# Hybrid decoder block: the attention values taken with the value block as weights, the probabilities scaled before they are turned, z multiplied ahead of the masks

## The reference, cut to what matters

```python
# attention: each query sees 128 keys back, plus one sink logit per head
scores = jnp.einsum('bnqgrd,bnkgd->bgrnqk', qb, kk)      # masked to the band
m      = jnp.maximum(jnp.max(scores, axis=-1, keepdims=True), sink)
pexp   = jnp.exp(scores - m)
probs  = pexp / (jnp.sum(pexp, axis=-1, keepdims=True) + jnp.exp(sink - m))
out    = jnp.einsum('bgrnqk,bnkgd->bnqgrd', probs, vv)
# SSD: y is the sum of a part within the chunk of 128 tokens and a part from the carried state
g = y * jax.nn.silu(z)                                   # z = u @ w_z
g = g * lax.rsqrt(jnp.mean(g * g, axis=-1, keepdims=True) + NORM_EPS)   # per group of 512
```

## Time and profile before

| | |
|---|---|
| median of 3 runs | 2165.03 us (2163.56 to 2168.50) |
| profiled execution | 2168.98 us, its span 2167.4 us |
| PE busy | 2090.6 us (96%) |
| VectorE / ScalarE / GpSimd busy | 1307.5 / 844.0 / 598.4 us |
| mean granted TensorE clock | 0.984 |
| `mixers` | 32 steps, 19.7 us each in the middle of a group |

### The profile page before, as it was taken

One profiled execution on the slowest core, in us unless ns is written; L12 is line 12 of the kernel. 1 busy time (PEld: TensorE's weight loads), 2 busy tenths in 40 slices (PEclk: granted clock), 3 DMA queues, 4 the chain that ended last, 5 costly groups with the idle time before them and its releaser, 6 DMA issues. The chain is left out here.

```text
span 2167.4 us, 29054 instructions
## 1 busy us (share of the span) xinstructions
PE 2090.6 (96%) x10218; PEld 1739.7 (80%) x10218; DVE 1307.5 (60%) x1824; ACT 844.0 (39%) x1589; POOL 598.4 (28%) x600
## 2 busy tenths in 40 slices
PE   7999999979999999999979999999999999999997
PEld 6888889967878778778758888887888888878885
DVE  6854552237767767777743344558887777752523
ACT  5332221024454444454443222434444443443432
POOL 1000011146576666565610000004222222100000
PEclk9999999989999999999989999999999999999998
DMA  6122241223443433443355434321222222355343
GB/s 225 62 90 97 87 166 69 84 85 129 119 125 117 124 114 124 124 131 97 95 175 179 141 134 145 122 94 72 88 87 71 75 87 87 138 161 195 112 151 88
DMA packets 131264, 252.73 MB, mean 117 GB/s; under 512 B 25264, under 2 KB 70448, under 8 KB 131152
## 3 DMA queue, kind: packets, MB, share of 16 engines
q1 hardware_dynamic: 85584, 174.98, 24.9%
q0 software_dynamic: 15360, 55.32, 7.5%
q10 hardware_dynamic: 30208, 20.98, 3.0%
HBM read 189.63 MB, written 61.60 MB: 116 GB/s over the span
## 5 line engine op out<-in xcount | busy, mean ns | idle before, releaser
L155 PE MATMUL ps_zg<-u_hi,g_hi 128*128 128x512 f32 x448 | 186.0, 415 | 0.0
L157 PE MATMUL ps_zg<-u_hi,g_lo 128*128 128x512 f32 x448 | 177.1, 395 | 0.0
L156 PE MATMUL ps_zg<-u_lo,g_hi 128*128 128x512 f32 x448 | 176.2, 393 | 0.0
L2057 DVE TENSOR_TENSOR lt_d_lo<-lt_w_raw,lt_d_hi 128x640 fp32r<-128x640 f32 (+1 forms) x64 | 57.1, 892 | 147.2 <-ACT lt_d_hi L1782 142.5
L973 POOL TENSOR_TENSOR mx_seg<-mx_seg,mx_cbm 128x1024 f32<-128x1024 f32 x32 | 76.0, 2376 | 161.3 <-DVE mx_cbm L1130 161.3
L155 PE MATMUL ps_zg<-z_w,u_hi 128*128 128x512 f32 x256 | 108.6, 424 | 7.1 <-DVE mx_silu L1155 6.9
L155 PE MATMUL lt_ps<-lt_h_hi,lt_w_hi 128*128 128x512 f32 x256 | 100.7, 393 | 14.8 <-DVE lt_h_lo L2095 13.6
L157 PE MATMUL ps_zg<-z_w,u_lo 128*128 128x512 f32 x256 | 102.3, 400 | 0.0
L156 PE MATMUL ps_zg<-z_w,u_hi 128*128 128x512 f32 x256 | 101.8, 398 | 0.0
L1782 ACT ACTIVATE lt_d_hi<-lt_w_raw 128x640 fp32r<-128x640 f32 (+1 forms) x64 | 50.6, 791 | 130.5 <-PE lt_ps L157 119.6
L1656 POOL TENSOR_TENSOR lt_t_f<-lt_w_raw 128x512 f32<-128x512 f32 x21 | 29.1, 1385 | 261.7 <-DVE lt_t_lo L1985 260.2
(11 more groups left out here) (390 smaller groups left out, 6229.8 us busy)
## 6 DMA issues: line engine op xcount, KB each, us to landing
lt_w_raw<-in_w_up SPq DMA_DIRECT2D x44, 512.0 KB, 4.5
mx_a_row<-acs_s SPq DMA_DIRECT2D x32, 512.0 KB, 3.9
g_raw<-in_w_xbc SPq DMA_DIRECT2D x24, 512.0 KB, 3.2
lt_sig<-gate_s SPq DMA_DIRECT2D x24, 512.0 KB, 3.6
lt_w_raw<-in_w_down SPq DMA_DIRECT2D x32, 384.0 KB, 3.2
ff_s<-lt_fo SPq DMA_DIRECT2D x21, 512.0 KB, 5.0
tok_s<-fr_work POOLq DMA_DIRECT2D x20, 512.0 KB, 3.8
lt_w_raw<-in_w_down SPq DMA_DIRECT2D x32, 320.0 KB, 2.9
```

The costliest lines, as they stand in the source:

```text
L155: pe.matmul(dst, s_hi, m_hi, start=first, stop=False)
L156: pe.matmul(dst, s_hi, m_lo, start=False, stop=False)
L157: return pe.matmul(dst, s_lo, m_hi, start=False, stop=last)
L2057: dve.tensor_tensor(d_lo[:, m % 2, 0:n], w_raw[:, m % 2, 0:n], d_hi[:, m % 2, 0:n].bitcast(F32), ALU.subtract).then_inc(dw_lo_done, 1)
```

## The change

The probabilities are scaled by `rden` before they are turned, by four ScalarE copies. So the product with the values needs no division afterwards, and it can be taken the other way round: the value block (64 columns) is the weights, two heads' turned probabilities (256 columns) the moving side, two such pairs go to the two halves of the partitions of `ps_f`, and what comes out is already turned. VectorE's `attention_out`, its tile `o_tok` and PE's L1261 go. The values stand behind gate 0 to 3 instead of ahead of it. The probabilities are turned after all of z instead of after z 2. On ScalarE the sigmoid's exp goes ahead of the splits and output copies; on VectorE silu(z) goes ahead of the gate split and the masks, and `rden` from behind the gated y to just behind the state update.

```diff
@@ ScalarE
-                act.wait_ge(o_turned, n + 1)
+                act.wait_ge(pv_done, n + 1)
...
                     act.activation(silu[:], silu[:], ACT.Ln, bias=one[:]).then_inc(z_ln_done, 1)
+                    act.wait_ge(z_ln_done, n + 1)
+                    act.activation(silu[:], silu[:], ACT.Exp, scale=-1.0).then_inc(z_sig_done, 1)
                     if c % 2 == 1 and not (last and c == NT - 1):
...
                         outputs(g if c else g - 1, (c - 1) % NT, first and c <= 2)
-                    act.wait_ge(z_ln_done, n + 1)
-                    act.activation(silu[:], silu[:], ACT.Exp, scale=-1.0).then_inc(z_sig_done, 1)
                     act.wait_ge(max_ready, n + 1)
                     keys = P if c == 0 else 2 * P
                     for r in range(REP):
-                        ins = act.activation(sc[:, r, 0:keys], sc[:, r, 0:keys], ACT.Exp, bias=negm[:, r:r + 1],
-                                             accum_out=sums[:, r:r + 1])
-                    ins.then_inc(exp_done, 1)
+                        act.activation(sc[:, r, 0:keys], sc[:, r, 0:keys], ACT.Exp, bias=negm[:, r:r + 1],
+                                       accum_out=sums[:, r:r + 1])
...
                         for k in range(4, KT):
                             split_z(g + 1, k)
+                    act.wait_ge(rden_ready, n + 1)
+                    for r in range(REP):
+                        ins = act.activation(sc[:, r, 0:keys], sc[:, r, 0:keys], ACT.Copy, scale=rden[:, r:r + 1])
+                    ins.then_inc(p_scaled, 1)
                     act.wait_ge(p_turned, n + 1)
@@ VectorE
-                    if not opening:
-                        attention_out(n - 1, first and c == 1)
...
                     dve.tensor_tensor(cbm[:], ps_d[:, 0:P], utri[:], ALU.mult).then_inc(cbm_ready, 1)
+                    dve.wait_ge(z_sig_done, n + 1)
+                    dve.tensor_tensor(silu[:], ps_z[:], silu[:], ALU.mult).then_inc(z_used, 1)
...
-                    dve.wait_ge(z_sig_done, n + 1)
-                    dve.tensor_tensor(silu[:], ps_z[:], silu[:], ALU.mult).then_inc(z_used, 1)
-
...
                         dve.tensor_tensor(state[:], kept[:], ps_f[:], ALU.add).then_inc(state_ready, 1)
+                    dve.wait_ge(sink_done, n + 1)
+                    if not opening:
+                        dve.wait_ge(p_scaled, n)
+                    do(dve.tensor_tensor(rden[:], sums[:], sink_e[:], ALU.add))
+                    dve.reciprocal(rden[:], rden[:]).then_inc(rden_ready, 1)
                     dve.wait_ge(diag_done, n + 1)
...
-                    dve.wait_ge(sink_done, n + 1)
-                    do(dve.tensor_tensor(rden[:], sums[:], sink_e[:], ALU.add))
-                    do(dve.reciprocal(rden[:], rden[:]))
@@ PE
+                n = NT * g + c
+                pe.wait_ge(p_ready, n + 1)
+                if c < NT - 1:
+                    pe.wait_ge(state_ready, (NT - 1) * g + c + 1)
+                else:
+                    pe.wait_ge(o_out, n)
                 j, blocks = c % 2, 1 if c == 0 else 2
-                for r in range(REP):
-                    for b in range(blocks):
-                        block_of = c if b == j else c - 1
-                        last = pe.matmul(ps_a[:, r * HD:(r + 1) * HD], p_t[:, r, b], v_in[:, block_of % 4],
+                for b in range(blocks):
+                    block_of = c if b == j else c - 1
+                    for h in range(2):
+                        last = pe.matmul(ps_f[h * HD:(h + 1) * HD, 0:2 * P].rearrange("p (a n) -> p a n", a=2),
+                                         v_in[:, block_of % 4], p_t[:, 2 * h:2 * h + 2, b],
                                          start=(b == 0), stop=(b == blocks - 1))
                 last.then_inc(pv_done, 1)
...
                     if not opening:
+                        gate(g, c, range(0, 4), opening)
                         values(*before)
-                    if not opening:
-                        gate(g, c, range(0, 4), opening)
...
-                    if not opening:
-                        pe.wait_ge(o_ready, n)
...
-                    next_z(g, c, last_group, range(0, 3))
-                    pe.wait_ge(exp_done, n + 1)
+                    next_z(g, c, last_group, range(KT))
+                    pe.wait_ge(p_scaled, n + 1)
                     for r in range(REP):
                         for b in range(keys // P):
                             last = pe.transpose(ps_s[:, r // 2, r % 2, b * P:(b + 1) * P], sc[:, r, b * P:(b + 1) * P], ident[:])
                     last.then_inc(p_turned, 1)
-                    next_z(g, c, last_group, range(3, KT))
```

More of the change, by code:

```diff
@@ L831, in mixers @@
         p_t = s.sb("p_t", [P, REP, 2, P])
-        o_tok = s.sb("o_tok", [P, REP * HD])
         o_t = s.sb("o_t", [P, 2, 2, P])
@@ L853, in mixers @@
             s.sem(n) for n in "gated sq_done v_ready r0_ready yn_ready y_turned y_out".split())
-        rotated, qk_turned, q_ready, scored, masked, max_ready, exp_done, sink_done, p_turned, p_ready, pv_done, o_ready, o_turned, o_out = (
-            s.sem(n) for n in "rotated qk_turned q_ready scored masked max_ready exp_done sink_done p_turned p_ready pv_done o_ready o_turned o_out".split())
+        rotated, qk_turned, q_ready, scored, masked, max_ready, sink_done, rden_ready, p_scaled, p_turned, p_ready, pv_done, o_out = (
+            s.sem(n) for n in "rotated qk_turned q_ready scored masked max_ready sink_done rden_ready p_scaled p_turned p_ready pv_done o_out".split())
         dve_own, pool_own, act_own = s.sem("dve_own"), s.sem("pool_own"), s.sem("act_own")
@@ L1096, in split_gate @@
                 dve.tensor_tensor(g_lo[:, w], g_raw[:, w], g_hi[:, w].bitcast(F32), ALU.subtract).then_inc(g_lo_done, 1)
-            def attention_out(n, opening):
-                dve.wait_ge(pv_done, n + 1)
-                if not opening:
[L1102 to L1106, removed]
             def group(g, first, last):
@@ L1194, in group @@
                 assert own.n == OWN
-            OWN = 8 * NT + 2 * (NT - 1) + (NT - 2)
+            OWN = 7 * NT + 2 * (NT - 1) + (NT - 2)
             group(0, True, False)
@@ L1200, in _ @@
             group(NG - 1, False, True)
-            attention_out(NG * NT - 1, False)
         @block.tensor
@@ L1236, in values @@
             def values(g, c):
-                pe.wait_ge(p_ready, NT * g + c + 1)
-                j, blocks = c % 2, 1 if c == 0 else 2
-                for r in range(REP):
-                    for b in range(blocks):
-                        block_of = c if b == j else c - 1
-                        last = pe.matmul(ps_a[:, r * HD:(r + 1) * HD], p_t[:, r, b], v_in[:, block_of % 4],
+                n = NT * g + c
[4 more added lines that the diff above has]
+                    pe.wait_ge(o_out, n)
+                j, blocks = c % 2, 1 if c == 0 else 2
+                for b in range(blocks):
[3 more added lines that the diff above has]
+                                         v_in[:, block_of % 4], p_t[:, 2 * h:2 * h + 2, b],
                                          start=(b == 0), stop=(b == blocks - 1))
@@ L1254, in turn_outputs @@
                 last.then_inc(y_turned, 1)
-                pe.wait_ge(o_ready, n + 1)
-                if c < NT - 1:
-                    pe.wait_ge(state_ready, (NT - 1) * g + c + 1)
-                else:
-                    pe.wait_ge(o_out, n)
-                for a in range(2):
-                    last = pe.transpose(ps_f[:, a * P:(a + 1) * P], o_tok[:, a * P:(a + 1) * P], ident[:])
-                last.then_inc(o_turned, 1)
             def group(g, first, last_group):
```

## The result

| | before | after |
|---|---|---|
| median of 15 runs each | 2167.25 us | 2172.40 us (2167.83 to 2176.61) |
| ratio, with its 95% interval | | 1.0024 (1.0017 to 1.0031), or +5.2 us |
| profiled execution, its span | 2168.98, 2167.4 us | 2170.32, 2168.7 us |
| PE busy | 2090.6 us | 2069.1 us |
| VectorE / ScalarE / GpSimd busy | 1307.5 / 844.0 / 598.4 us | 1251.8 / 887.5 / 595.4 us |

The kernel is slower by 5.2 us, where 8.4 had been forecast, while TensorE is busy for 21.5 us less. A second measurement of the same kernel gave 1.0019 (1.0010 to 1.0028), or +4.1 us. The two profiled executions differ by only 1.3 us of span. A second profiled execution of the changed kernel had a span of 2173.6, +6.2.

A forecast was written before the change was run, and what follows sets the result against it. TensorE was taken as the bound in the middle of a group, 19.74 us a step. Terms of -4.8, -0.6, +1.3, +9.0 and +3.5 gave +8.4 on a median of 2165.03, so 2173.4 us; range 2160 to 2191.

The forecast's parts named there:

- 12 even steps: Even steps in the middle of a head group take 19.27 us, 0.4 less than now: -4.8 us together.
- 12 odd steps: Odd steps take 19.8 us against 19.85, with `rden` held up by GpSimd's decays: -0.6 us together, bounds 19.3 and 20.9.
- 3 first steps: In each group's first step the scores come later and only half the values go: +0.45 us each, +1.3 together.
- 3 last steps of a group: VectorE's low halves of z 4 to 7 come later, TensorE idles some 6 us: +3.0 each, bounds 1 and 5.
- the end, less the first step: The last step, with no z to hide anything, is 4.3 us later; less 0.8 for the first step: +3.5.
- The values: On TensorE, eight records of 256 columns in two column halves take 1.15 us instead of 1.70; bounds 0.86 and 2.0.
- The chain ahead of the scores: From transposes through norm, decays and copies of q and k, scores start at 7.17; TensorE waits 0.35 us every step.
- the sign that the chain is shorter than I read: Steps at 19.0 us in the profile after would show the forecast wrong about the wait ahead of the scores.
- rival B: In odd steps GpSimd's loads land 1 us later and `rden` meets only short operations: -5.7 us, 2159.3; chance 0.14.
- rival D: Chain ahead of the scores 0.3 shorter (even steps 18.97), last steps of a group +2: +1 us, 2166; chance 0.13.

The follow-up runs named there:

- run 1: Changed kernel with both head pairs sent to partitions 0 to 63, so the column halves can't work side by side: 2185.13 us, ratio 1.0083.
- Run 4: Changed kernel with the decays' clamp ahead of the previous step's norm and their exp behind its square: 2159.68 us, ratio 0.9956.
- run 10: Kernel before with only the four-column maximum operations in PSUM, the sink sum staying in SBUF: 2164.22 us, ratio 0.9986.
- run 6: Changed kernel with the maximum of the scores and the sink's exponential held in PSUM: 2158.41 us, ratio 0.9968.
- run 8: Changed kernel with the decays' clamp and exp done a step early, and the maximum and sink's exponential in PSUM: 2143.66 us, ratio 0.9890.

## Why the prediction was right, and where it was not

The forecast was +8.4 (2173.4 us), in a range of 2160 to 2191; the time came out at 2172.4 (+5.2), and at +4.1 in the second measurement. The reason given was that TensorE's gain in the loop is eaten by the group ends and the end. That is what the tables show. Term by term, with the first trace:

| term | forecast | measured |
|---|---|---|
| 12 even steps | -4.8 | -8.4 |
| 12 odd steps | -0.6 | -5.1 |
| 3 first steps | +1.3 | +0.4 (second trace +2.8) |
| 3 last steps of a group | +9.0 | +9.7 |
| the end, less the first step | +3.5 | +4.4 |
| sum | +8.4 | +1.0 (second trace +4.6) |

- *The values* were put at 1.15, with 0.86 and 2.0 as ends; they take 1.02. The analogy to the scores' two halves held, and run 1 shows what it was worth: 0.85 a step.
- *The chain ahead of the scores* was the right bound. It was to be 7.17 from the transposes and is 7.03 (546.35 - 539.32): the copy to `p_t` starts 0.06 earlier (540.39), and the clamp follows it after 3.69 (544.08), not 3.76. Behind the scores it is 11.95 for 12.1. So even steps are 18.97 instead of 19.27; the announced idle ahead of the scores was 0.35, and is 0.11 to 0.15. I had named 19.0 as the sign that the chain is shorter than I read, and so it is, by 0.14. Run 4 took the chain away and found the 0.2.
- *Odd steps* are the term that failed: -0.05 forecast, -0.42 measured. The step of the working that was wrong is the start of the masks, 10.55 after the gate. I took the 4.04 from q's copy to the masks from the earlier trace rows, and in them lies VectorE's gate split as it ran beside GpSimd. In the new order GpSimd's mix has ended (8.2 after the gate) when the split begins, and it takes 1.23 instead of 1.98. First the rows of before (GpSimd and VectorE, the step of the earlier trace rows), then those of after, an odd step from 559.09:

```profile
687.39 2.38 POOL L973 TENSOR_TENSOR mx_seg<-mx_seg,mx_cbm 128x1024 f32<-128x1024 f32 x1 [4.57 <-DVE mx_cbm L1130]
...
688.87 1.98 DVE L1096 TENSOR_TENSOR g_lo<-g_raw,g_hi 128x1024 fp32r<-128x1024 f32 x1 [1.62 <-ACT g_hi L1018]
```

```profile
564.91 2.38 POOL L972 TENSOR_TENSOR mx_seg<-mx_seg,mx_cbm 128x1024 f32<-128x1024 f32 x1 [2.92 <-ACT mx_seg L1028]
...
566.58 0.69 DVE L1122 TENSOR_TENSOR mx_silu<-ps_zg,mx_silu 128x512 f32<-128x512 f32 x1 [2.30 <-ACT mx_silu L1039]
567.53 1.23 DVE L1098 TENSOR_TENSOR g_lo<-g_raw,g_hi 128x1024 fp32r<-128x1024 f32 x1 [0.26 <-ACT g_hi L1017]
568.67 1.28 DVE L1132 SCALAR_TENSOR_TENSOR mx_sc<-mx_ps_s,band 128x512 f32<-128x512 f32 x2
...
574.35 0.16 DVE L1160 TENSOR_TENSOR mx_rden<-mx_sums,mx_sink_e 128x4 f32<-128x4 f32 x1 [0.32 <-ACT mx_sink_e L1053]
...
574.95 1.91 POOL L954 TENSOR_TENSOR mx_seg<-mx_a_row,mx_acs_g 128x1024 f32<-128x1024 f32 x1
```

  Masks start 9.58 after the gate, and `rden` at 15.26 (16.4 forecast), with GpSimd's decays at 15.86. The sum gets through 0.6 us ahead of the decays, and takes 0.16. This is rival B's place, and nearly its gain (-5.1 against -6.6), though not by its mechanism: GpSimd was no later than I had put it (decays at 16.2 after the gate; they came at 15.0 to 16.1), but VectorE was earlier. It is a near miss: in seven of the twelve steps the sum starts less than 0.1 us ahead of the decays, and in three more it starts behind them and takes 1.25 to 1.30.
- *Group ends* had the right size, +3.25 each on average for +3.0 (2.6, 2.1 and 5.0), from partly other parts. Halves at 19.5 (20.6 forecast, less the one microsecond by which the masks came sooner); 5.07 long, not 3.00, which I had taken from the earlier trace rows without asking what GpSimd would do beside them by then; and an idle of 5.2 for 6 in the step shown, of which 1.76 stands ahead of L1284 and not ahead of z 4, where all 6 had been put. What I had missed altogether is why they are late. I knew the collision of small operations from the earlier trace rows and looked for it at `rden` only; the maximum's two operations had it in the step of the earlier trace rows already, and my working moved it along unseen. It cost 5.7 us at the three group ends of the kernel before (run 10) and costs 9.7 in the changed one (run 6), whose group ends without it take as long as those of the kernel before (73.70 and 73.63).
- *The end*: the last transposes start 15.96 after their gate, against 11.23, so 4.7 later for 4.3. Most of the rest of the 0.9 over the forecast is the transposes at the lower clock, 1.79 for 1.09. The slow values cost nothing: they end at 1101.81, and TensorE's next work, the turn of y, starts at 1102.58, when VectorE's norm is done.

That the total landed within 3.2 us of the forecast is in part luck. Steps c = 0 to 6 gained 9.0 more than the terms gave them (-13.1 for -4.1), while the group ends and the end lost 1.6 more. By the first trace the sum is rival D's (+1.0), and D's chain, 0.3 shorter, is what the even steps show, though not its +2 at the group ends. The medians lie between D and the forecast. Part of the gap between trace and median is which executions were profiled: that of before lies 1.7 above its median (2168.98 for 2167.25), the first of after 2.1 below (2170.32 for 2172.40), the second 5.1 above (2175.17 for 2170.07). Why executions of one kernel differ is only partly seen. The second trace is 3.6 longer than the first in the table, and steps n = 16 and n = 9 alone are 3.7 longer (21.00 for 18.65, 21.94 for 20.62). In n = 16 TensorE waits 2.29 ahead of the scores, in the first trace not at all. I have no run that fixes how far GpSimd and VectorE have come when that step starts.

## What to carry to other kernels

When work moves off the bounding engine, list each wait that it used to cover, with the chain that will end last there; here TensorE was busy for 21.5 us less and the program got slower, until two such chains were shortened; with them shortened the same change was worth about 20 us (runs 8 and 10). A duration taken from a row carries the neighbours that ran beside it: ask of each what GpSimd did then, and what it will do in the new order, for tiny operations above all. Cures found one at a time need not go together: the two reorderings that made 3 us with a late maximum cost 6.6 with an early one.

## What the runs showed of the hardware

- A VectorE `tensor_tensor` on 128x4 with both inputs in SBUF took 0.16 us or up to 1.85 us, by GpSimd's operation beside it, and a `tensor_scalar` 0.17 or up to 1.21; with one operand in PSUM they always took 0.15 to 0.17 (runs 6 and 8). The low half of the gate weights (128x1024) took 1.23 clear of GpSimd's mix and 1.98 where it met it. The row maximum over 128x1024 took 1.22 either way.
- The clock multiplies a wait. After 3.48 us idle, z 4 to 7 took 5.65 at a granted clock of 0.52, against 3.19 at 1.00 in run 8. It is not a matter of the longest idle alone: in run 6 a group's end with one idle of 1.75 had a mean clock of 0.85. In run 8 one with 2.32 and 0.93 had 1.00, and the next one, with 2.33 and 0.93, had 0.93. What decides between these can't be said from these traces.
- Eight fp32 matmuls with 64 columns of weights and 256 moving columns take 1.02 us in two column halves and 1.87 in one (run 1), which is 1.83 times as long; both times are from the first record to the next operation.
